# A four-layer decoder step on one core: an opening whose loads are joined, cache pages that arrive turned, and state copies moved behind weight loads

## What is computed

```python
sh1p, sc1p, g1p, sh2p, sc2p, g2p = adaln(c_prompt, ada_w[i], ada_b[i])
hp = modulate(xp, norm1_g[i], sh1p, sc1p)          # rms_norm(x, g) * (1 + scale) + shift
...
xp = xp + g1p * yp
xp = xp + g2p * sq_relu_mlp(modulate(xp, norm2_g[i], sh2p, sc2p), mlp_w1[i], mlp_w2[i])
```

```python
def page_part(phys):
    k_nope, v, kpe = mla_expand(cache[phys], w_kvb, g_kn)
    sc = mla_scores(q_nope, q_pe, k_nope, kpe)
    m = sc.max(axis=-1)
    e = jnp.exp(sc - m[..., None])
    return m, e.sum(axis=-1), jnp.einsum('nhsk,nkhd->nhsd', e.astype(v.dtype), v).astype(jnp.float32)
```

## Time and profile before

| | |
|---|---|
| median of 3 runs | 2162.27 us (2161.82 to 2162.92) |
| profiled execution | 2162.28 us, span 2160.6 us |
| TensorE (PE) busy | 1966.2 us, 91% |
| VectorE (DVE) busy | 1126.0 us, 52% |
| ScalarE (ACT) busy | 788.5 us, 36% |
| GpSimd (POOL) busy | 24.0 us, 1% |
| read from device memory, written | 391.23 MB, 60.28 MB |

### The profile page before, as it was taken

How to read it: one execution, slowest core, us unless ns; L and a number is a source line. 1 busy time by engine, 2 the same in 40 slices (tenths; PEclk the granted TensorE clock), 3 DMA queues, 4 the chain that set the end, 5 groups by cost and what they waited for, 6 DMA issues and landing times.

```text
span 2160.6 us, 32785 instructions
## 1 busy us (share of the span) xinstructions
PE 1966.2 (91%) x13076; PEld 1685.6 (78%) x13076; DVE 1126.0 (52%) x1910; ACT 788.5 (36%) x1557; POOL 24.0 (1%) x44
## 2 busy tenths in 40 slices
PE   4798799999998788999969999897889999789997
PEld 1685699989996557999839999753588888679997
DVE  1552654448945346544385544577545545365532
ACT  1420443234533224432234432342344545144422
POOL 0000000000000000000000000000000000000000
PEclk9899899999997999999979999996799999799999
DMA  6764755663442796656555666521036867434442
GB/s 236 265 247 153 249 204 208 212 234 103 135 147 117 313 366 224 210 200 214 186 200 200 209 211 218 173 86 47 1 111 214 264 214 247 145 101 153 156 142 78
DMA packets 213234, 399.28 MB, mean 185 GB/s; under 512 B 7864, under 2 KB 194143, under 8 KB 196193
## 3 DMA queue, kind: packets, MB, share of 16 engines
q1 hardware_dynamic: 209552, 332.68, 44.4%
q0 software_dynamic: 2384, 60.28, 8.3%
q10 hardware_dynamic: 1161, 4.34, 0.6%
HBM read 391.23 MB, written 60.28 MB: 209 GB/s over the span
## 4 chain that ended last, share of the span: by engine, by line
PE 81%; DVE 9%; DMA 5%; ACT 2%; issue 1%; ACTq 0%; SPq 0%; POOL 0%; DVEq 0%; POOLq 0%
PE bank L1120 40%; PE bank L1026 10%; PE bank L1509 8%; PE bank L1039 5%; PE bank L1095 4%; PE bank L991 2%; PE bank L1207 2%; DVE rstd L1763 2%; DMA work<-in_keys_turned 2%; DMA work<-in_ada_w 1%; PE bank L1539 1%; PE bank L1085 1%; DMA ring<-in_mlp_w 1%; PE bank L1244 1%; DVE ring_lo L1630 1%
## 5 line engine op out<-in xcount | busy, mean ns | idle before, releaser
L1630 DVE TENSOR_TENSOR ring_lo<-ring,ring_hi 128x1024 fp32r<-128x1024 f32 (+1 forms) x324 | 380.2, 1214 | 367.8 <-ACT ring_hi L672 367.7
L672 ACT ACTIVATE ring_hi<-ring 128x1024 fp32r<-128x1024 f32 (+1 forms) x324 | 323.1, 1046 | 333.9 <-PE bank L1120 279.6
L1120 PE MATMUL bank<-hidden_hi,ring_hi 128*128 128x320 f32 x1024 | 318.9, 311 | 0.0
L1120 PE MATMUL bank<-hidden_hi,ring_lo 128*128 128x320 f32 x1024 | 316.4, 309 | 0.0
L1120 PE MATMUL bank<-hidden_lo,ring_hi 128*128 128x320 f32 x1024 | 316.3, 309 | 0.0
L1120 PE MATMUL bank<-h_hi,ring_hi 128*128 128x320 f32 x896 | 279.6, 312 | 0.1
L1120 PE MATMUL bank<-h_lo,ring_hi 128*128 128x320 f32 x896 | 276.2, 308 | 0.0
L1120 PE MATMUL bank<-h_hi,ring_lo 128*128 128x320 f32 x896 | 275.9, 308 | 0.0
L1120 PEld LDWEIGHTS bank<-hidden_hi,ring_hi 128*128 128x128 f32 x1024 | 192.2, 188 | 20.1 <-issue 20.1
L1120 PEld LDWEIGHTS bank<-hidden_lo,ring_hi 128*128 128x128 f32 x1024 | 192.3, 188 | 0.0
L1120 PEld LDWEIGHTS bank<-hidden_hi,ring_lo 128*128 128x128 f32 x1024 | 192.2, 188 | 0.0
(11 more groups left out here) (279 smaller groups left out, 3273.7 us busy)
## 6 DMA issues: line engine op xcount, KB each, us to landing
ring<-in_mlp_w SPq DMA_DIRECT2D x128, 1024.0 KB, 5.4
work<-in_ada_w SPq DMA_DIRECT2D x88, 1024.0 KB, 7.5
ring<-in_swa_w_qkv SPq DMA_DIRECT2D x18, 1024.0 KB, 5.1
out_swa_old<-in_state_swa POOLq DMA_DIRECT2D x8, 2016.0 KB, 9.6
ring<-in_conv_w_in SPq DMA_DIRECT2D x12, 1024.0 KB, 6.8
work<-in_keys_turned SPq DMA_DIRECT2D x8, 1280.0 KB, 12.8
work<-in_cache_mla SPq DMA_DIRECT2D x64, 160.0 KB, 2.2
ring<-in_ada_w SPq DMA_DIRECT2D x8, 1024.0 KB, 12.0
```

The costliest lines, as they stand in the source:

```text
L672: act.activation(ring_hi[:, place, part], ring[:, s, part], ACT.Copy).then_inc(sem("weights_hi"), 1)
L1120: mm = pe.matmul(bank[a % 4][:, 0:T], w[:, k, :], x(k), start=first and k == 0 and j == 0, stop=last and k == KD - 1 and j == 2)
L1630: dve.tensor_tensor(ring_lo[:, s, part], ring[:, s, part], ring_hi[:, place, part], ALU.subtract)\
```

## The change

1. **Opening.** The tables are loaded in two parts (the identity, ones and eps first), the vectors in two groups (4 early, 12 late); the convolution's state goes behind the early ones. Of layer 0's eight modulation pieces four go into the ring (`ADA_MAIN`), the others into the side slots (`load_first`). TensorE turns x between modulation steps; the root and reciprocal of the first norm come ahead of the first split, and of the convolution's units only unit 0 is split ahead of the norm.
2. **Gaps.** SP loads side units between the weight units of the first MLP instead of five in a row ahead of them. GAP_SIDES is 3; 18 side units instead of 16 (`SIDE_BEHIND`) lie behind MLP units. In a norm the root comes ahead of the second half of unit 1's `ring_hi`, VectorE makes the sample columns of `h_lo` for several pieces at once, and unit 1's `ring_lo` comes at k = 4 instead of k = 1.
3. **MLA.** The host hands the cache over three times: page rows, pages turned and the rotated part turned, and the key expansion turned. The device loads them ready; `page_turn`, the 16 turns and ScalarE's copies of them go. The new latent rows are stored turned. Per sequence there are 24 page transfers instead of 8, and the split pages lie in a ring of four.
4. **State copies.** Five sequences' copies stay in the decode; the last three are issued in the last MLP, when the units `mlp1_3` + 1, + 9 and + 17 are done.

```diff
+ADA_MAIN = 4
...
-SIDE_LAYER0 = (SIDE_PARTS - 1) * KD
+SIDE_FIRST = KD - ADA_MAIN
+SIDE_LAYER0 = SIDE_FIRST + (SIDE_PARTS - 1) * KD
 SIDE_LAYER = SIDE_PARTS * KD
-GAP_SIDES = 4
+GAP_SIDES = 3
 GAP_FIRST = 1
+SIDE_BEHIND = sorted([*range(0, 32, 2), 7, 23])
+ROLL_DECODE = 5
...
-            for k in range(KD):
-                load(k, k % RING, 1, SIDE_COLS, ada[0, k:k + 1, :, 0:SIDE_COLS].rearrange("k p n -> p k n"), first=k < RING)
-            def load_side(l, x):
-                v = side_no(l, x)
+            for k in range(ADA_MAIN):
+                load(k, k % RING, 1, SIDE_COLS, ada[0, k:k + 1, :, 0:SIDE_COLS].rearrange("k p n -> p k n"), first=True)
+            def side_slot(v):
                 if v >= SIDE:
                     sp.wait_ge(sem("side_done"), v - SIDE + 1)
+            def load_first(v):
+                side_slot(v)
+                sp.dma_start(side[:, v % SIDE, :], ada[0, ADA_MAIN + v, :, 0:SIDE_COLS]).then_inc(sem(f"side_landed{v % SIDE}"), 16)
...
+                    if l == 0 and u < 3:
+                        for v in (((0, 15),), ((1, 0), (1, 1)), ((1, 2),))[u]:
+                            load_side(*v)
...
                     for x in range(SIDE, 2 * SIDE):
                         load_side(l + 1, x)
-                elif u >= RING and u % 2 == 0:
-                    load_side(l + 1, GAP_SIDES + u // 2)
-                if u in (29, 31):
-                    load_side(l + 1, SIDE_LAYER - GAP_SIDES + (u - 29) // 2)
+                if u - RING in SIDE_BEHIND:
+                    load_side(l + 1, GAP_SIDES + SIDE + SIDE_BEHIND.index(u - RING))
...
+            def turned_pages(n):
+                half = n % 2
                 for j in range(PAGES):
+                    phys, landed_here = page_number(n, j), sem(f"pages_{'first' if j < 4 else 'last'}_landed{half}")
+                    sp.dma_start(md_lT[half][:, j, :, :], A["pages_turned"][bass.ds(phys, 1)].rearrange("a p c k -> (a p) c k"))\
+                      .then_inc(landed_here, 16)
+                    r = ROPE * (j % 2)
+                    sp.dma_start(md_rT[half][r:r + ROPE, j // 2, :], A["pages_rope"][bass.ds(phys, 1)].rearrange("a r k -> (a r) k"))\
+                      .then_inc(landed_here, 16)
+            def page_rows(n):
+                for j in range(PAGES):
+                    phys = page_number(n, j)
+                    sp.dma_start(md_pg[n % 2][:, j, 1:PG], A["pages_rows"][bass.ds(phys, 1)].rearrange("a p e -> (a p) e"))\
+                      .then_inc(sem(f"page_rows_landed{n % 2}"), 16)
+            for n in range(NS):
+                if n == 1:
+                    sp.wait_ge(sem("mla_prompt_done"), 1)
+                if n >= 2:
+                    sp.wait_ge(sem("md_latents_split"), PAGES * (n - 1))
+                    sp.wait_ge(sem("md_keys"), PAGES * (n - 1) + 1)
+                turned_pages(n)
+                if n >= 2:
+                    sp.wait_ge(sem("md_pv"), n - 1)
+                page_rows(n)
             mlp(3)
...
+                with gp.Fori(0, ROLL_DECODE) as n:
                     gp.wait_ge(sem("md_scored"), n + 1)
-                    for g in range(G):
-                        rows, lost = SWA_KEEP[g], SWA_KEEP[g] - SWA_OLD[g]
-                        gp.dma_start(O[f"swa{g}_old"][bass.ds(n, 1)].rearrange("n l k h d -> (n l) (k h d)"),
-                                     A[f"state_swa{g}"][0, bass.ds(n, 1), lost:rows].rearrange("n l k h d -> (n l) (k h d)"))\
-                          .then_inc(sem("stored"), 16)
+                    roll_sequence(n)
+                for n in range(ROLL_DECODE, NS):
+                    gp.wait_ge(sem("unit_done"), UNIT0["mlp1_3"] + 8 * (n - ROLL_DECODE) + 1)
...
+            squares(0, range(KD))
+            norm_std(0)
+            weights_hi("conv_in", 0)
+            norm(0, split=True)
+            weights_hi("conv_in", 1)
...
-                act.wait_ge(sem("md_turned"), PAGES * n + j + 1)
-                ins = act.activation(lT_parts[0][:, :, j, :], bank[6][:, 0:2 * P].rearrange("p (c k) -> p c k", c=2), ACT.Copy)
-                if j == 4:
-                    if n:
-                        act.wait_ge(sem("md_read"), n)
-                    ins = act.activation(md_new[0:TS].rearrange("p a x -> p (a x)"), bank[6][0:TS, 384:512], ACT.Copy)
-                if j % 2 == 0:
-                    ins = act.activation(md_rT[:, j // 2, :], bank[6][:, 2 * P:3 * P], ACT.Copy)
-                ins.then_inc(sem("md_latents"), 1)
+                k, half = PAGES * n + j, n % 2
+                if j in (0, 4):
+                    act.wait_ge(sem(f"pages_{'last' if j else 'first'}_landed{half}"), 128 * (n // 2 + 1))
+                if k >= 4:
+                    act.wait_ge(sem("md_keys"), k - 2)
+                act.activation(lT_parts[0][:, :, k % 4, :], md_lT[half][:, j, :, :], ACT.Copy).then_inc(sem("md_latents"), 1)
...
+            pe.wait_ge(sem("x_landed"), 32)
+            turn_x(0)
+            turn_x(1)
+            pe.wait_ge(sem("silu_ready"), 1)
+            for k in range(ADA_MAIN):
+                weights(k)
+                modulation(0, k, ring[:, k % RING, :]).then_inc(sem("unit_done"), 1)
+                turn_x(2 + k)
+            turn_x(KD - 2)
+            turn_x(KD - 1)
+            pe.wait_ge(sem("vecs_landed"), 16 * VEC_DMAS)
+            for t in range(2):
+                mm = turn(bank[6][:, t * P:(t + 1) * P], vec_in[:, t, :], P)
+            mm.then_inc(sem("start_turned"), 1)
+            def first_side(v):
+                pe.wait_ge(sem(f"side_landed{v % SIDE}"), 16 * (v // SIDE + 1))
+                modulation(0, ADA_MAIN + v, side[:, v % SIDE, :]).then_inc(sem("side_done"), 1)
+            for v in range(SIDE):
+                first_side(v)
             pe.wait_ge(sem("x_copied"), KD)
             norm(0, split=True)
-            pe.wait_ge(sem("silu_ready"), 1)
+            pe.wait_ge(sem("conv_state_landed"), 16)
+            pe.wait_ge(sem("late_vecs_landed"), 16 * LATE_VEC_DMAS)
+            pe.wait_ge(sem("start_read"), 1)
             for k in range(KD):
-                weights(k)
-                modulation(0, k, ring[:, k % RING, :]).then_inc(sem("unit_done"), 1)
-            pairs("conv_in", 12, KD, ni=0, each=lambda u: side_unit(0, u))
+                mm = turn(bank[6][:, 2 * P + k * 16:2 * P + (k + 1) * 16], cv_in[0:2 * NS, k * P:(k + 1) * P], 2 * NS)
+            turn(bank[6][:, 3 * P:3 * P + 64], vec_in[0:64, 2, :], 64).then_inc(sem("start_turned"), 1)
+            for v in range(SIDE, SIDE_FIRST):
+                first_side(v)
+            def after_conv_in(u):
+                if u == 0:
+                    pe.wait_ge(sem("start_read"), 2)
+                side_unit(0, u)
...
-                side_unit(0, 12 + u)
+                for x in ((12, 13), (14,), (15,), ())[u]:
+                    side_unit(0, x)
...
-            def page_turn(n, j):
-                k, half = PAGES * n + j, n % 2
-                if j in (0, 4):
-                    pe.wait_ge(sem(f"pages_{'last' if j else 'first'}_landed{half}"), 64 * (n // 2 + 1))
-                if k:
-                    pe.wait_ge(sem("md_latents_split"), k)
-                if j == 4:
-                    for c in range(2):
-                        pe.matmul(bank[6][0:TS, 384:448], ml_lat[:, c, TP:T], md_q[:, c, n, :, :].rearrange("p h s -> p (h s)"),
-                                  start=c == 0, stop=c == 1)
-                    pe.matmul(bank[6][0:TS, 448:512], ml_rope[:, TP:T], md_qr[:, n, 0, :], start=True, stop=True)
-                for c in range(2):
-                    mm = turn(bank[6][:, c * P:(c + 1) * P], md_pg[half][:, j, 1 + c * P:1 + (c + 1) * P], P)
-                if j % 2 == 0:
-                    turn(bank[6][0:ROPE, 2 * P:3 * P], md_pg[half][:, j, 1 + LORA:PG], P)
-                    mm = pe.matmul(bank[6][ROPE:P, 2 * P:3 * P], md_pg[half][:, j + 1, 1 + LORA:PG], ident, start=True, stop=True)
-                mm.then_inc(sem("md_turned"), 1)
...
+                if j == 4:
+                    for c in range(2):
+                        pe.matmul(bank[6][0:TS, 384:448], ml_lat[:, c, TP:T], md_q[:, c, n, :, :].rearrange("p h s -> p (h s)"),
+                                  start=c == 0, stop=c == 1)
...
-            page_turn(0, 0)
             for k in range(NS * PAGES):
                 n, j = divmod(k, PAGES)
-                if k + 1 < NS * PAGES:
-                    page_turn(*divmod(k + 1, PAGES))
...
                 sample(slice(0, 2))
-                for k in range(KD):
+                prompt(0)
+                prompt(1)
+                if split:
+                    low(0)
+                    low_sample(slice(0, 2)).then_inc(sem("h_split"), 1)
+                sample(slice(2, KD))
+                if split:
+                    low(1).then_inc(sem("h_split"), 1)
+                for k in range(2, KD):
                     prompt(k)
-                    if k == 1:
```

(47 more changed lines are left out.)

205 lines of the change are left out of this document (107 added, 98 removed).

## The result

The changed kernel takes 2140.35 us (median of four runs, 2138.6 to 2145.16) against 2162.43; the ratio is 0.9902, with a 95% interval of 0.9889 to 0.9914. It is faster by 1%, 22 us, where 68 were forecast: the time lies 26 us above the range. The profiled execution took 2138.6 us with a span of 2136.8, 23.8 less than before.

What follows compares the result with a forecast made beforehand. TensorE's chain of waits (81%) was taken as the bound, with savings only where it stands or does other work. Terms -22.9 + 0.5 - 11.7 - 3.3 - 4.0 + 6.0 - 5.7 - 29 + 2 gave -68.1: 2094 us, range 2080 to 2114.

Steps and rivals of the forecast that it cites:

- Opening: Start up to the first product: x and modulation wait only for their own loads, -22.9 us (bounds -27 and -17).
- First gap: Convolution to first MLP: alternating weight and side loads bring the last update earlier (-14.2); -11.7 us in all.
- the side unit (+1.0): Gap ahead of the first MLP: a side unit of 1.07 us now stands on the path, +1.0 us.
- the late split (+0.5): Convolution: unit 1's split of weights now follows the norm, +0.5 us.
- +2.4 for the restart: First MLP's start: TensorE stands there and restarts at its lower clock, +2.4 us.
- -0.9 for h_lo: First MLP's second product group: its 1.19 us wait for h_lo shrinks through VectorE's new order, -0.9 us.
- Other gaps and sides: Later norm gaps: fewer side units -3.3, table loads and h_lo waits -4.0, sides moved behind MLP units +6.0 us.
- Decode, the turns: Decode: page turns leave TensorE, -3.6 us per sequence, -29 in all (bounds -22 and -34).
- Decode, the transfers: Decode: SP's 24 page-load issues per sequence need some 24 us and fit; pages 27 to 30 us after issue still in time.
- Copies in the last MLP: Last MLP: three state copies beside the weight loads cost +2 us for all three (bounds 0 and +17).
- The rival: Weights and pages starve behind the copies: last MLP +5.8 us per copy, +17 for three, 2108 us; chance 0.17.
- The case with both failures at once: Combinations of two rivals, in decode or last MLP, which the forecast left outside its range of 2080 to 2114 us.

Runs made afterwards that it cites:

- the experiment with one piece ahead: Changed kernel, with VectorE in a norm making piece k + 1 of h before taking the low part of piece k; 2132.88 us, ratio 0.9858.

## Why the prediction was wrong
**Opening**: right, to 0.6 us, in mechanism and terms.

**First gap**: the mechanism was right, the agreement to 0.2 us is luck in part. From the end of the convolution's last product to the first product of the MLP it was 23.1 us and is 9.1, -14.0 where -14.2 was forecast. The convolution ahead of it got 3.0 us longer, where the side unit (+1.0) and the late split (+0.5) were to make it 1.5. So what belongs to this row was forecast as -12.7 and came to -11.0; the other +2.4 for the restart and -0.9 for h_lo act behind the first product, in the next row of the table.

**Other gaps and sides** (-3.3, -4.0, +6.0 on four MLPs' surroundings): the direction of the parts was right, the terms of the gain too large. In front of layer 1 the gap went from 10.4 to 7.8 us. But the first two units behind it now take 16.6 us where they took 15.8, since VectorE's new order hands pieces over every 1.45 us. The -0.9 per norm for the h_lo wait was counted without the wait that takes its place; the experiment with one piece ahead got about that much back per norm (15.7 us for these two units).

**Decode, the turns**: right in mechanism, too small in size. Without copies the decode takes 235.9 instead of 271.0, -35.1, where -29 was forecast, and beyond the bound of -34. It is 29.5 us per sequence where 30.8 was forecast. The wait of the turned maximum, which was to grow by 0.2 to 0.5, fell from 0.44 us to 0.17.

**Decode, the transfers**: the first step that failed, "SP then needs some 24 us for 24 issues; they fit". The 24 us are right for a round without a copy (24.1), but SyncE's issues stand still for some 10 us while a copy runs, so a round took 34.5 with one copy and 47.3 with two. I had asked when a page lands and whether that is early enough; it was, with 22.6 us at most, inside the 27 to 30 that I allowed. I had not asked whether the queue can still issue the transfers behind it. Against TensorE's 29.7 the lateness is 4.8 us in a round with one copy and 17.6 in one with two, and it adds up until the lead is used. Copies cost the decode 17 us with five of them and 36 with eight. What an issue waits for inside those 10 us no run shows; with the copies in 4 KB packets the stand is gone.

**Copies in the last MLP**: the second step that failed, the term of +2, which measured +31. Without copies this row is -0.6, so they cost 31.6. The rival named the mechanism and had 0.17, but was priced too low as well, 5.8 per copy (its own terms, 27 less 21.4, give 5.6). The waits alone were 8.3 per copy, 10.3, 8.1 and 6.4, with the other 6 us in slow restarts, which the rival left out. From a load's issue to the product it feeds it was 27.5 to 29.2 us and not 27, and the first load was needed after 18.3 us already, the others after 21.1. With packets of 64 KB against 1.0 KB the load gets almost nothing until the copy ends, some 24 us after its issue; the queued loads then move together, and the first landed 26.2 us after its issue, not 24.8. "The transfer engines are not full in an MLP", my argument against, is a mean over time and says nothing about the time of a copy, in which they are (100% from 1888 to 1898). Averages of the whole profile gave 25 KB and 1.6 KB, a ratio of 16; in the stretch it was 64. A slip besides: a copy is 6.75 MB (53.9 MB less on the copies' queue for eight), not 7.5.

Whether the two queues share by packets or by bytes was called open, with "No row here has both queues loaded long enough to show it". That was wrong: the trace of the kernel before has such a stretch in the attention, where stores of new keys and values on GpSimd's queue meet loads of old values on SyncE's. From 650 to 653 us:
```profile
q0 software_dynamic: 111, 1.01, 79.1%
q1 hardware_dynamic: 109, 0.20, 17.2%
```
The packet counts are equal to 2%, and the bytes differ by a factor of five. The size of the copies' packets could be read there as well: from 1650 to 1660, beside nothing else,
```profile
q0 software_dynamic: 63, 3.60, 108.1%
```
Eight of the 63 have under 512 bytes, the others 65 KB each. These two rows speak for the rival that had 0.17. The case with both failures at once had been left out of the range as a combination of two rivals. Both come from the copies' large packets, so they were not independent.

## What to carry to other kernels
Before a large transfer is moved beside loads, compare the packet sizes of the two queues in the very stretch: with one packet each in turn, a stream of small packets keeps only its part of the pair's bytes. If that is below its need, the burst must be shorter than the loads' lead, or cut into smaller packets. A change that shortens a stage also takes away cover: what was free beside 34 us of work, here the copies, must be counted again beside 30, with the issuing queue's own time per round and what stops it. Rivals that share a cause belong into the range together.

## What the hardware showed that was not expected
- Two queues with work got 50 and 49 packets in 10 us, and 1017 and 1004 in 14 us, at 64 and 3.8 KB against 1.0 KB; in the kernel before 111 and 109 in 3 us, at 9 KB against 1.8 KB.
- A transfer's issue on SyncE took 10.1 us instead of 0.48 while another queue's copy ran, and at most 1.64 when that copy had 4 KB packets (1.35 with all eight copies in the decode).
- Pieces of 1 KB instead of 2 KB left the copies' packets at 3.8 KB, from 4.0; cutting a contiguous copy into eight parts made them 17.6 KB on average, from 60.
